# RWKV's front in four steps: the squares of the keys stand three groups ahead of their total and root

## What is computed

```
kk = heads(k * f32(k_k))
kk = kk / jnp.maximum(jnp.sqrt(jnp.sum(kk * kk, axis=-1, keepdims=True)), 1e-12)
k = k * (1.0 + (a - 1.0) * f32(k_a))
...
y = wkv7_scan(r_h, w_h, k_h, v_h, -kk, kk * a_h)
```

## Time and profile before

| | us |
|---|---|
| median of 3 runs (2111.15 to 2112.51) | 2111.76 |
| the profiled execution, its own time | 2110.7 |
| its span, first to last instruction | 2108.8 |
| PE busy in the span | 2033.7 (96%) |
| DVE busy | 990.4 (47%) |
| ACT busy | 781.4 (37%) |
| POOL busy | 292.6 (14%) |
| fronts and cores, 180 to 500 us: PE, DVE, ACT, POOL busy | 303.7, 160.7, 69.8, 61.8 |

### The profile page before, as it was taken

How to read it: one execution, slowest core, us unless ns; L and a number is a source line. 1 busy time by engine, 2 the same in 40 slices (tenths; PEclk the granted TensorE clock), 3 DMA queues, 4 the chain that set the end, 5 groups by cost and what they waited for, 6 DMA issues and landing times.

```text
span 2108.8 us, 27562 instructions
## 1 busy us (share of the span) xinstructions
PE 2033.7 (96%) x11518; PEld 1629.0 (77%) x11518; DVE 990.4 (47%) x1534; ACT 781.4 (37%) x1233; POOL 292.6 (14%) x292
## 2 busy tenths in 40 slices
PE   7998999999999999999899999998999999999996
PEld 5766767777888778888677788886788888888884
DVE  5665554544553233336855444446643432333354
ACT  5573221223444333234524243335322343322344
POOL 2001121210221001012300000001310220100124
PEclk9999998999999999999999999998999999999997
DMA  5121111111633332322421222221232233322221
GB/s 181 55 70 61 45 48 42 46 47 51 220 100 103 107 103 95 100 93 95 143 90 52 69 71 80 80 90 60 80 100 92 98 125 106 100 98 97 96 80 50
DMA packets 59843, 185.46 MB, mean 88 GB/s; under 512 B 6551, under 2 KB 11799, under 8 KB 59592
## 3 DMA queue, kind: packets, MB, share of 16 engines
q1 hardware_dynamic: 59720, 183.71, 26.2%
HBM read 173.46 MB, written 10.22 MB: 87 GB/s over the span
## 4 chain that ended last, share of the span: by engine, by line
PE 87%; DVE 4%; ACT 4%; issue 2%; POOL 1%; DMA 1%; SPq 0%; DVEq 0%; POOLq 0%; ACTq 0%
PE P L547 25%; PE P L549 24%; PE P L548 24%; DVE AREN L1651 1%; PE P L822 1%; PE P L858 1%; PE P L912 1%; PE P L851 1%; PE P L910 1%; PE P L807 1%; DVE WLO L1658 1%; POOL AREN L2323 1%; DVE AREN L1654 1%; PE P L1035 1%; DVE AREN L1791 1%
## 5 line engine op out<-in xcount | busy, mean ns | idle before, releaser
L547 PE MATMUL P<-HH,WHI 128*128 128x512 f32 x1528 | 624.6, 409 | 22.4 <-DVE WLO L1658 12.2
L549 PE MATMUL P<-HH,WLO 128*128 128x512 f32 x1528 | 603.7, 395 | 0.0
L548 PE MATMUL P<-HL,WHI 128*128 128x512 f32 x1528 | 602.8, 394 | 0.0
L1106 ACT ACTIVATE WHI<-RAW 128x1024 fp32r<-128x1024 f32 x303 | 318.9, 1053 | 443.9 <-PE P L549 440.8
L1658 DVE TENSOR_TENSOR WLO<-RAW,WHI 128x1024 fp32r<-128x1024 f32 x303 | 381.7, 1261 | 150.1 <-ACT WHI L1106 148.8
L547 PEld LDWEIGHTS P<-HH,WHI 128*128 128x128 f32 x1528 | 291.0, 190 | 100.4 <-issue 15.4
L547 PE MATMUL P<-ARR,WHI 128*128 128x512 f32 (+1 forms) x904 | 351.7, 389 | 7.6 <-DVE AREN L1651 2.9
L549 PE MATMUL P<-ARR,WLO 128*128 128x512 f32 (+1 forms) x904 | 350.1, 387 | 0.0
L548 PE MATMUL P<-ARR,WHI 128*128 128x512 f32 (+1 forms) x904 | 350.1, 387 | 0.0
L549 PEld LDWEIGHTS P<-HH,WLO 128*128 128x128 f32 x1528 | 291.1, 190 | 63.3
L548 PEld LDWEIGHTS P<-HL,WHI 128*128 128x128 f32 x1528 | 291.4, 191 | 55.9 <-issue 0.2
(11 more groups left out here) (297 smaller groups left out, 1553.1 us busy)
## 6 DMA issues: line engine op xcount, KB each, us to landing
RAW<-in_w_in_dram SPq DMA_DIRECT2D x118, 512.0 KB, 3.3
RAW<-in_w_ff_dram SPq DMA_DIRECT2D x64, 512.0 KB, 3.3
RAW<-in_w_ml_dram SPq DMA_DIRECT2D x64, 512.0 KB, 3.2
RAW<-in_w_out_dram SPq DMA_DIRECT2D x16, 512.0 KB, 3.3
RAW<-in_w_pg_dram SPq DMA_DIRECT2D x16, 512.0 KB, 3.3
AREN<-in_xT_dram SPq DMA_DIRECT2D x16, 256.0 KB, 6.4
s_gates<-AREN SPq DMA_DIRECT2D x16, 256.0 KB, 2.0
RAW<-in_w_ab_dram SPq DMA_DIRECT2D x8, 512.0 KB, 3.4
```

Source lines behind the costliest of these rows:

```text
L547: e.matmul(out, hi, H[0][:, s], start=first, stop=False)
L548: e.matmul(out, hi, H[1][:, s], start=False, stop=False)
L549: return e.matmul(out, lo, H[0][:, s], start=False, stop=last)
L1106: e.activation(WHI[n % NSPL][:, :], RAW[n % NRAW][:, :], ACT.Copy).then_inc(*D.act.sig("whi", n))
```

## The change

The front gets a fourth step. The first keeps kk, kp and the square. PE's total (ss), DVE's maximum and ACT's root become the second step, BK, the product with the root and ba the third, and a, b and POOL's share the fourth. The second step stands behind lb4 of the quarter before, so three core groups (lb3, la4, lb4) stand between the square and its total. The list gets one group more at its start, which moves most core groups by one or two dense rows.

```diff
@@ weave_order
-    seq = [["f"], ["f"], ["f"]]
+    seq = [["f"], ["f"], ["f"], ["f"]]
     for what, q, lev in core_steps():
-        seq.append(["c"] + (["f"] if q < 3 and (what in "WN" or (what, lev) == ("la", 3)) else []))
+        seq.append(["c"] + (["f"] if q < 3 and (what in "WN" or (what, lev) in (("la", 3), ("lb", 4))) else []))
@@ tensor_program, front
                 for q in range(4):
+                    yield
                     b = 6 + jj
                     w.wait_ge(F.act.at("sq", q), free.get(b))
                     e.matmul(bank(b)[:, 0:256], cst("bones"), p_.B["tmp"], start=True, stop=True).then_inc(
@@ pool_program, front
-                    yield
-                    yield
+                    for _ in range(3):
+                        yield
```

## The result

| | before | after |
|---|---|---|
| median of 4 runs each, us | 2111.45 (2109.63 to 2112.51) | 2091.09 (2086.11 to 2093.60) |
| ratio of after to before, 95% interval | | 0.9914 (0.9887 to 0.9941) |
| repeated later: 11 and 6 runs | 2106.03 (2099.73 to 2112.05) | 2090.49 (2087.66 to 2095.11) |
| its ratio | | 0.9926 (0.9906 to 0.9945) |
| profiled execution: own time, span | 2110.7, 2108.8 | 2093.17, 2091.3 |

The change is faster by 0.7 to 0.9%, 15 to 20 us; 13.7 were forecast.

A forecast was written before the change was run, and what follows sets the result against it. PE, busy for 96% of the span, was taken as the bound. Won 11.9 + 1.4 + 4.2 + 1.7 = 19.2 us, less 2.2, 0.5 and 2.8, is 13.7: median 2098.1 us, 8 in 10 range 2092 to 2106.

The forecast's parts named there:

- (a): The seven later waits of ss, PE's total, for ACT's square: 1.65 us each from start to start, 11.9 us won.
- (b): The first wait of ss, 1.81 us, gets two dense rows more ahead: 1.4 us won, 0.4 stays.
- (c): PE's other waits, at N 1.2, G 0.6, la1 0.8, the variance's root 1.0 and M 0.6: 4.2 us won.
- (d): The granted clock's fall behind the first wait of ss doesn't come any more: 1.7 us won.
- (e): What is late next: la1 of pair 1 behind DVE's burst at pair 0's quarter 1, 2.2 us; M 0.5; collisions 2.8.
- M's 0.5: In row 265, Ln, Exp and the variance's root precede ACT's copies of pair 1's W: a wait of M, 0.5 us.
- the 0.6 of M that were to stay: M's waits for ACT's copies with one dense row between W and M: three places become two, 0.6 us stay.
- The collisions: New small PE waits as new pairs of instructions collide, between none and as many as today's again: 2.8 us lost.
- (1): Rival: the waits move, DVE's burst at every la3 meeting an add that PE needs; 7.1 us won, 2104.7; chance 0.10.
- (2): Rival: both pairs' O's, one dense row apart, make one longer clock fall; 6.8 us go, 2104.9; chance 0.07.
- (3): Rival: DVE becomes the bound of the chunks, six bursts costing 2.2 each; 6.7 us slower, 2118.5; chance 0.04.

The follow-up runs named there:

- the list alone: The kernel before with only an empty group at the head of its list, so its groups stand where the change has them; 2107.29 us, ratio 1.0000.
- the experiment with the add in W: The change, with GpSimd's add of lnx_b to the bonus moved from lb3 to behind its two products in W; 2086.62 us, ratio 0.9892.

## Why the prediction was right, and where it was off

The direction, the mechanism and most sizes held. By its own steps:

(a), (b) ss. "11.9 us won" and "1.4 won, 0.4 stays", less la1's 2.2, is 11.1; ss alone measured 10.8 ± 1.4, set right 11.8 ± 0.9. The first wait left 0.45, and no later one is left.

(c) The other waits. The size held: 4.2 were forecast, and the list alone takes 4.3 us of idle time away, 4.8 ± 1.5 at full clock, set right 3.5 ± 0.9. How it was split did not. 1.2 (N) was put on the early root, but the list alone removes N's wait as well, and the early root adds nothing to it. The step is "Now the root is taken in lb4, and DVE's k, root's product and ba need nothing that is late, so this goes: 1.2". In the earlier trace rows the mix and the WLO tile stood behind ba and ahead of M's adds, and the list moved both away. Whether the early root would do the same on the old list isn't shown; DVE's 4.27 idle us would have been there for these two. What the root does bring, about 3 us, is at the G's of quarter 0. The prediction put G's 0.6 on the list, rightly, as the list alone shows, but didn't see that with ss in a step of its own both G's would wait without the early root (1.16 and 0.77).

(d) The clock. At 183 to 190 us it stayed at 1.00, as forecast, but not by the reason given alone. With ss back in the first step the same wait of 1.81 us stands there and the clock stays high (the first line); with the list alone it falls (the second):

```profile
186.00:188.00 2.00, 2.00 (x11) 1.00 0.66 244
186.00:188.00 2.00, 2.00 (x6) 0.50 0.01 2
```

So of three traces with that wait two show the fall, of nine without it none. Over all runs the change lost 35.0 us to the clock against 36.5, which is 1.5 beside the 1.7 said, with an interval of ± 3, so the agreement of the two numbers may be luck.

(e) la1's new wait was forecast as 2.2 at this place and is 2.15. Both sides were 0.4 longer than said: from L840's start DVE was done at +4.1 instead of +3.75, as GpSimd's operations lay beside both of kp (0.95 and 0.72 us), and PE came at +2.0 instead of +1.6. M's 0.5 is one wait of 0.58, at quarter 0 of pair 1 (298.8 us) and not in row 265. With the 0.6 of M that were to stay, 1.1 was expected there, so 0.5 less came.

The collisions are the term that was mis-sized: 2.8 was allowed, and one wait of 0.19 us arose, with the 0.2 of L791 that stood before too. Net without the clock the forecast was 12.0; 15.2 was measured, ± 0.9 (set right 15.6). These 2.6 and the 0.5 above are 3.1 of the 3.2 between them.

The rivals: in (1), waits of 1 to 2 us at every la3, there is one, so it fell. (2) priced the closer O's at 6.8. In the change the fall around them is as long as before (0.57 over 16 us, beside 0.60 over 17), and its runs lost no more time, 35.0 beside 36.5. So nothing of this rival is seen in the change. The list alone, with the same distance, did lose 5.1 us more than the kernel before, and no run says whether the O's did that. (3) fell with (1): DVE's burst makes a matmul wait for 2 us at one of six places. The page TensorE: Matmul & The Clock Gate (Part 1) of the Trainium skill, by which low clock follows idle time, is borne out in part: behind the first ss and behind la1 the clock fell only where PE had stood for 1.8 us or more, in five of nine such cases, but 306 to 322 us has PE busy for 16.00 of 16 at 0.57.

One reading was wrong without cost. The prediction took kk's 0.42 beside GpSimd's add as evidence against a shared interface. kk had started 0.16 us before the add, and kp's first operation, which started 0.17 behind the add's start, took 0.41 us more than alone. At the second place GpSimd was still busy with an earlier product, until 258.63, when kk started at 258.39, and there kk too took 0.52 instead of 0.42. The Trainium skill (SBUF — State Buffer, Who interferes with whom, and the section on its two sides) says that VectorE with two SBUF inputs and GpSimd hold the shared ports for a whole instruction, whoever starts first. The trace agrees on who is held: the operation that starts second is lengthened, and in the experiment with the add in W the lengthening goes with the add.

## What to carry to other kernels

Where the program of each engine is one list, the first thing to look for is a matmul that needs a chain of two other engines begun in its own step; give it a few groups of other work between, and count each removed wait as its idle time and 0.2 to 0.4 us beside it. Then look at what that engine's idle time gave others: the same list position that freed ss made la1 wait for VectorE. Test such changes on the order alone too: here a shift of one or two dense rows, with no step changed, was worth a quarter to a third of the gain at full clock, though in time its runs gave it back to the clock.

## What the runs showed of the hardware

- The granted clock falls to 1.2 GHz at places that differ between runs of one kernel: behind the same wait of 2.15 us the change had 0.72 over 6 us in one trace and 0.50 in its repeat, and a kernel with the same order there 1.00. One fall cost 1.7 us before (184 to 190 us, 6 us at 0.72 in the mean), the one around the O's after 6.9 (16 us at 0.57, PE busy throughout). Together they are 30 to 42 us in the mean of a kernel's runs, and 25 to 51 in a single run, counted as span less span times clock.
- Span times granted clock told kernels apart that differ by 3 us, where medians of a dozen runs didn't (the list alone, 2107.29, beside 2108.33 for 29 runs of the kernel before, with 4.8 us won at full clock). It counts about a quarter too much for the clock, and it says nothing of what an edit does to the clock itself.
- A VectorE operation of 0.42 us with two inputs in SBUF took 0.83 to 0.95 beside a GpSimd operation that had begun before it. With that one moved away it took 0.42, in the change's six cases in five; in the sixth another GpSimd operation still stood beside it (0.95).
- A wait of a matmul can cost more than the idle time that the profile shows. From start to start ss stood 2.00 us behind the bonus with 1.30 shown as idle, where a pair without a wait takes 0.35. Over the whole change 15.3 ± 0.9 us were won at full clock for 12.7 us less idle time in 164 to 500 us and eleven waits fewer, 0.2 to 0.3 each. For the waits of ss alone it is 3.0 ± 0.9 us beyond the idle time in five waits, for those that the list removed nothing (3.5 ± 0.9 won for 4.3 us less idle, both set right). So it is seen where ss waited and isn't shown for every matmul.
